# Weight splits as one instruction of 2048 columns in place of two of 1024, in a two-block transformer kernel

## The reference

```python
proj = h @ w_in
x = x + mixed @ w_out
q = h @ w_q;  k, v = split(mem_n @ w_kv);  x = x + o @ w_o
val, gate = split(h @ w_up);  x = x + (silu(conv(gate)) * val) @ w_down
proj = h @ w_in_2;  kc = gelu(flat @ w1) @ w2
x = x + (g_a * (o_a @ w_pa) + g_b * (o_b @ w_pb)) @ w_o_2
x = x + square(relu(h @ w_up_2)) @ w_down_2
```

## Time and profile before

| | |
|---|---|
| median of 3 runs | 2813.39 us (2812.67 to 2813.58) |
| the profiled execution | 2813.74 us |
| its span, first to last instruction | 2812.0 us |
| mean granted TensorE clock | 0.998 |
| low-part instructions of VectorE (L217) | 968, 1093.0 us busy |
| high-part instructions of ScalarE (L211) | 968, 933.8 us busy |
| DMA | 519.61 MB, mean 185 GB/s |

### The profile page before, as it was taken

The page is one execution under the profiler, slowest core; times in us unless marked ns, Lnnn a source line. Parts: engine busy times, 40 slices in busy tenths (PEclk is TensorE's granted clock), DMA queues, the critical chain, the costliest instruction groups (busy, mean ns, idle before and its releaser), DMA issues.

```text
span 2812.0 us, 36427 instructions
## 1 busy us (share of the span) xinstructions
PE 2783.2 (99%) x14439; PEld 2371.5 (84%) x14439; DVE 1714.9 (61%) x2311; ACT 1348.8 (48%) x1961; POOL 53.2 (2%) x97
## 2 busy tenths in 40 slices
PE   8999999999999999999999999999999999999998
PEld 6888888888888888888888888888888888888887
DVE  5666666566664667665566687456656654456554
ACT  5455555554443444455555475445444333334343
POOL 1001000000000000000100000000000000000000
PEclk9999999999999999999999999999999999999999
DMA  7445445455555555555664444336555555555553
GB/s 289 153 160 200 177 166 176 148 199 184 193 165 194 210 190 185 171 181 208 228 236 150 150 153 177 122 133 262 180 185 190 188 201 194 194 191 185 193 195 135
DMA packets 78700, 519.61 MB, mean 185 GB/s; under 512 B 9624, under 2 KB 9840, under 8 KB 24272
## 3 DMA queue, kind: packets, MB, share of 16 engines
q1 hardware_dynamic: 71648, 487.73, 49.5%
q0 software_dynamic: 6896, 29.70, 2.9%
HBM read 508.98 MB, written 12.35 MB: 185 GB/s over the span
## 4 chain that ended last, share of the span: by engine, by line
PE 94%; DVE 2%; ACT 2%; issue 1%; DVEq 1%; DMA 0%; ACTq 0%; SPq 0%
PE acc L318 19%; PE acc L320 19%; PE acc L319 19%; PE wk L396 15%; PE wk L402 8%; PE acc L396 5%; PE acc L402 2%; DVE w_lo L217 1%; PE wk L944 1%; PE wk L914 1%; ACT w_hi L211 1%; PE wk L2707 1%; PE wk L640 1%; PE wk L2716 1%; PE wk L766 1%
## 5 line engine op out<-in xcount | busy, mean ns | idle before, releaser
L217 DVE TENSOR_TENSOR w_lo<-w_raw,w_hi 128x1024 fp32r<-128x1024 f32 x968 | 1093.0, 1171 | 792.0 <-ACT w_hi L211 790.0
L211 ACT ACTIVATE w_hi<-w_raw 128x1024 fp32r<-128x1024 f32 x968 | 933.8, 1013 | 1088.9 <-PE acc L320 656.3
L318 PE MATMUL acc<-w_hi,h 128*128 128x512 f32 x1120 | 451.7, 403 | 3.7 <-DVE w_lo L217 3.5
L396 PE MATMUL wk<-h,w_hi 128*128 128x512 f32 x1824 | 440.5, 390 | 0.0
L320 PE MATMUL acc<-w_hi,h 128*128 128x512 f32 x1120 | 439.1, 392 | 0.0
L319 PE MATMUL acc<-w_lo,h 128*128 128x512 f32 x1120 | 438.6, 392 | 0.0
L396 PEld LDWEIGHTS wk<-h,w_hi 128*128 128x128 f32 x1824 | 337.5, 188 | 66.9
L318 PE MATMUL acc<-w_hi,f_hi 128*128 128x512 f32 x856 | 334.0, 390 | 1.4 <-DVE sums L376 1.0
L319 PE MATMUL acc<-w_lo,f_hi 128*128 128x512 f32 x856 | 333.2, 389 | 0.0
L320 PE MATMUL acc<-w_hi,f_lo 128*128 128x512 f32 x856 | 333.2, 389 | 0.0
L318 PEld LDWEIGHTS acc<-w_hi,h 128*128 128x128 f32 x1120 | 211.8, 189 | 47.7 <-DVE w_lo L217 4.3
(11 more groups left out here) (441 smaller groups left out, 2650.7 us busy)
## 6 DMA issues: line engine op xcount, KB each, us to landing
w_raw<-in_w_up_a SPq DMA_DIRECT2D x76, 1024.0 KB, 4.8
w_raw<-in_w_up_b SPq DMA_DIRECT2D x72, 1024.0 KB, 4.7
w_raw<-in_w_win SPq DMA_DIRECT2D x68, 1024.0 KB, 4.8
w_raw<-in_w_merge SPq DMA_DIRECT2D x32, 1024.0 KB, 4.8
w_raw<-in_w_down_a SPq DMA_DIRECT2D x32, 1024.0 KB, 4.8
w_raw<-in_w_down_b SPq DMA_DIRECT2D x32, 1024.0 KB, 4.8
w_raw<-in_w_win2g SPq DMA_DIRECT2D x24, 1024.0 KB, 4.8
w_raw<-in_w_down_a SPq DMA_DIRECT2D x24, 768.0 KB, 4.2
```

What stands on the lines that cost most here:

```text
L211: act_.activation(w_hi[:, s % SPL, a:b], w_raw[:, s % RAW, a:b], ACT.Copy).then_inc(hi_ready, 1)
L217: dve_.tensor_tensor(w_lo[:, s % SPL, a:b], w_raw[:, s % RAW, a:b], w_hi[:, s % SPL, a:b].bitcast(F32), ALU.subtract).then_inc(lo_ready, 1)
L318: pe_.matmul(o, xh, wh, start=kt == 0, stop=False)
L396: pe_.matmul(self.sets[n % 2][m][:, 0:2 * S], w_hi[:, s, c:c + P], h[:, kt0 + k, :, :].rearrange("p a b -> p (a b)"), start=kt0 + k == 0, ...
```

## The change

From the fifth item on, each item's high part is one instruction over all its columns (2048, 1536 or 1024), and so is its low part. The semaphores go up by two at once. The low part waits for the whole high part. What TensorE and the loads wait for is unchanged in the code: the same counts of `lo_ready`, both of which now come at the end of the one instruction. The first four items stay as they were.

```diff
+            def whole(self, n, j):
+                return not (isinstance(n, int) and self.b + n * self.ipc + j < RAW)
+
             def make_hi(self, e, n, j):
...
+                if self.whole(n, j):
+                    act_.activation(w_hi[:, s % SPL, 0:self.cols(j)], w_raw[:, s % RAW, 0:self.cols(j)],
+                                    ACT.Copy).then_inc(hi_ready, 2)
+                    return
                 for a, b in self.parts(j):
                     act_.activation(w_hi[:, s % SPL, a:b], w_raw[:, s % RAW, a:b], ACT.Copy).then_inc(hi_ready, 1)
 
             def make_lo(self, e, n, j):
                 i, s = self.b + n * self.ipc + j, self.slot(n, j)
+                if self.whole(n, j):
+                    e.wait_ge(hi_ready, i * 2 + 2)
+                    dve_.tensor_tensor(w_lo[:, s % SPL, 0:self.cols(j)], w_raw[:, s % RAW, 0:self.cols(j)],
+                                       w_hi[:, s % SPL, 0:self.cols(j)].bitcast(F32),
+                                       ALU.subtract).then_inc(lo_ready, 2)
+                    return
                 for p, (a, b) in enumerate(self.parts(j)):
                     e.wait_ge(hi_ready, i * 2 + p + 1)
```

## The result

The changed kernel takes **2872.61 us** (median of 4 runs, 2870.77 to 2872.90) against 2813.17 us (4 runs): a ratio of 1.0211, 95% interval 1.0194 to 1.0227. It is 59 us slower; 2858 (2838 to 2880) was forecast. The profiled execution took 2870.77 us with a span of 2869.0 us, 57.0 more than before, where 44.3 were forecast. The direction, the mechanism and most of the places came out as forecast; the sum is 12.7 us short, and the experiments split that. One sign that the prediction had named against itself did appear: the granted clock fell in three new places.

A forecast was written before the change was run, and what follows sets the result against it. TensorE, busy 99% of the span, was taken to bound the kernel, so every delay reaching it is paid in full. Terms 14.2 + 6.9 + 10.1 + 13.9 = 45.1, less about 0.8, gave +44.3 us: 2858 us (2838 to 2880).

The forecast's parts named there:

- One sign that the prediction had named against itself: Anywhere in the kernel: the prediction is wrong if the granted clock falls in new places.
- Prices: 2048-column instructions, by the slope between 512 and 1024 columns: 1.92 us on ScalarE, 2.29 us on VectorE.
- Hidden in full items: Long runs of full items: some 400 items cost nothing, the item before hiding the split with 0.88 us to spare.
- Term 1: down_a and down_b: 16 3-tile items behind 2-tile items stall 0.84 us each, third items add 0.4 twice; +14.2 us.
- Term 2: Compression: 2048-column items with short cover stall at every other item, four stalls of 1.72 us; +6.9 us.
- Term 3: Ten single places in down2_b, win2, up_b, merge, pa and win: stalls of 0.39 to 1.88 us; +10.1 us.
- Term 4: Mostly attention stages: VectorE results queued behind a low part reach TensorE up to 0.82 us later, 19 places; +13.9 us.
- The 0.8 won back: Items directly behind a stall win back about 0.8 us, taken off the sum of the terms.
- its rival in small: Some 15 stalls each draw TensorE's clock down to 1.2 GHz; about 2885 us; with longer chains, chance 0.08.
- What would show it: Signs in the trace: w_lo waits from 3.9 to some 35 us, other waits up some 14 us, TensorE's busy time unchanged.

The follow-up runs named there:

- long_only: Whole instructions only in up_a, wo, up2_a, down2_a and up2_b, pairs everywhere else as in the kernel before; 2813.50 us, ratio 1.0003.
- inc1: The changed kernel, but each whole instruction steps its semaphore by one, with the awaited counts rewritten; 2861.32 us, ratio 1.0176.
- first_only: Whole instructions only in the first stage, win from its fifth item to co, pairs elsewhere as in the kernel before; 2829.57 us, ratio 1.0061.
- hi_only: The changed kernel, but only ScalarE's high part is whole (step of two); VectorE's low part stays a pair with steps of one; 2848.90 us, ratio 1.0130.
- pairs_inc2: The kernel before, two instructions for each part, but each steps its semaphore by two, with all counts doubled; 2813.79 us, ratio 1.0005.
- cut_512: The kernel before, two instructions with steps of one, but cut behind the first 512 columns instead of in the middle; 2821.42 us, ratio 1.0040.

## Why the prediction came out as it did

**Prices: right.** 1915 and 2292 ns against 1.92 and 2.29 us. The Trainium skill's page ScalarE: Activation LUTs, section What ACT_TABLE_LOAD costs, gave 1.89 us, and an estimate by its terms for 1536 columns is 1.47; the rows have 1915 and 1488 ns, so the row's slope was the better base.

**Hidden in full items: right.** The stages that the prediction names there hold 252 items, though, not some 400. The long stages moved by 0.1 us, and 0.9 us in the timed runs of `long_only`, within what can be told.

**Term 1, down products, +14.2: too small, 19.1 measured.** The 16 stalls stood where forecast. What was wrong is the size of one: 0.84, measured as 1.02 (the mean shift of these items between the two traces). The sum of the path lacked 0.07 us between high and low part and 0.02 between TensorE and high part, both from the step by two (in `inc1` the shift is 0.96). The last 0.1 is neither: matmuls right behind a stall start 0.33 us apart instead of 0.23, and the forecast had them at full pace. Third items: 0.51 and 0.54, forecast 0.4. Not seen at all: the fifth item of each chunk of down_b, 0.12 to 0.18 each, and the first item of down_a's next three chunks, 0.37 each, where an evacuation (L2106) stands behind the longer low part.

```profile
859.86 0.19 PEld L331 LDWEIGHTS acc<-w_hi,f_hi 128*128 128x128 f32 x1 [0.50 <-DVE x L2106]
```

**Term 2, compression, +6.9: right, 7.6.** Four stalls at every other item, 1.9 each with the slow matmuls behind it.

**Term 3, ten single places, +10.1: right where it can be read.** up_b 0.8 (0.79), merge 2.6 clean (2.2), pa 1.4 (1.39), down2_b 2.2 (1.83). The stall of 1.88 us in win2 was mis-added: by its own row it is 4.30 less 2.36, 1.94. In win2 two terms meet: 4.35 forecast for the stage, 4.6 in `inc1`. In the changed kernel the place worked out as 1.88 gave only 0.37, because the slow clock just ahead (1375.5) made the item before it longer, and so the cover: the stretch cost 1.7 us there and hid 1.5.

**Term 4, queued results, +13.9: the right kind, 10 to 20% too small.** From win to co 11.4 were forecast, with win's 0.39 of term 3 11.8; `first_only` gives 14.1 clean and `inc1` 13.0. That it is results and not low parts, the traces show: in those stages TensorE's matmuls wait 10.5 us more in the changed kernel (16.9 to 27.4), and only 0.3 of it for low parts. The delay itself was given as 0.82 us, where 4.25 less 3.45 is 0.80; the ends measured are 4.31 and 3.46, so 0.85. Second attention's start 1.7, measured 1.8 in z. Missed: win2g, 0.5 to 1.0. That the middle between zero and double came out so close is partly luck, since only one of its some 19 places was laid open. `hi_only` shows that these stages see the end of the low part alone.

**The 0.8 won back:** no such place was found; the 0.8 adds to what was too small.

**The 12.7 us that were missing** are then: 3.3 net of two more stretches at 1.2 GHz, 3.3 for the steps of two, and 6.1 in places (2.9 in the down products, 1.2 from win to co, the rest spread). Each of the first two is good to about 1 us only. The second is a step that the prediction did not have: it costed the instructions and left the changed semaphore step at nothing. The first is its rival in small: slow clock did follow some of the lengthened stalls of 1.5 to 2.0 us. The rival, together with longer chains, had a chance of 0.08, at 26 us and more; the net here is 3.3. The prediction had also named a clock that falls in new places as a sign of being wrong. The sign appeared, so its picture of the clock was wrong, while its time held, because each such stretch cost only 1.65 us and there were two more, not 15.

**What would show it.** The waits of TensorE's matmuls for low parts were forecast to rise from 3.9 to some 35 us; at the same line they are 31.2 (28.1 and the 3.1 of the program's start), and 32.9 with L409. Its waits for everything else were to rise by some 14 us, and rose by 12.1. Low parts start 2.02 us behind the start of high parts, not 1.95, for the step of two. "TensorE's busy time unchanged" was wrong: 16.5 us more, from the slow clock and the slow matmuls behind stalls (with one stretch, in `inc1`, it is still 7.7 more).

**The rule weighed against it.** The Trainium skill, in Perfetto Trace Analysis, section Optimizing Scalar/DVE Operations, says that breaking instructions up may let work finish sooner where these engines aren't saturated but leave bubbles elsewhere. The traces agree in both directions: merging cost 59 us, a cut into four won 7.8. They also show where it ends: eight parts lose most of that again.

## What to carry to other kernels

Where one engine prepares a buffer for the next, cost a change of its instructions by when the last byte is ready behind the event that frees the buffer, against the cover at the shortest item, and not by busy time: here the engines got 30 and 47 us cheaper and the kernel 59 us slower. Look at everything queued behind the longer instruction as well; with ScalarE's instruction alone whole that was 13 of 33 us. In a pipeline of two engines finer cuts let the second follow closely and shorten the whole, until what each further instruction adds eats it: four parts of 512 columns were best here, at 2805 us, and back-to-back low parts take 2.36 us in two, 2.50 in four and 2.80 in eight.

## What the runs showed of the hardware

**A semaphore step of two costs a separate wait.** With a step of one, wait and step stand on the compute instruction itself; with a step of two the trace has an instruction of its own on the engine's sequencer for the wait, just ahead (the changed kernel has 657 such on VectorE, the kernel before 179; on ScalarE, where many waits stood alone already, 621 against 571). The compute instruction then starts 0.102 us behind the releasing instruction's end instead of 0.032 on VectorE, and 0.118 instead of 0.097 on ScalarE behind TensorE. `inc1` (179 and 571 such waits, and 0.032 and 0.097 us again) and `pairs_inc2` show that it is the step and not the length. In `hi_only`, where only ScalarE's instruction steps by two, ScalarE starts late (0.119 us) and VectorE doesn't (0.033): what counts is the step of the instruction that waits.

**TensorE's first matmuls behind a stall are slower,** with the granted clock still at 2.4 GHz: the second starts 0.33 us behind the first instead of 0.23, and a whole item takes 0.10 to 0.13 us longer. What causes it is open.

**The clock falls behind some idle stretches and not behind others.** Idle stretches of 1.51, 1.68 and 1.98 us were followed, 0.8 to 1.3 us behind their ends, by a stretch at 1.2 GHz; 1.89 us in `inc1` had none, nor had 1.6 to 1.7 us four times in the compression of the changed kernel, nor 2.57 us in win2 in `inc1`. At the place where the kernel before had 2.74 us and then the slow clock, `pairs_inc2` had 2.89 us and kept its clock. And the stretches in merge came with no idle time over 0.3 us in the 5 us ahead of them. The count in the profiled runs differs (three before, five in the changed kernel, two with eight parts, one with four parts, none with `cut_512` or `pairs_inc2`), but the two in merge came and went in kernels with the same program there, so no rule follows from these runs.
